# Thirty-two expert weights in 18 passes instead of 20: two passes of four experts, a pair at the end

## The reference, cut to what matters

```python
w_pair = g_w * jax.nn.softmax(top_v, axis=-1)        # two weights per token
e_id = g_sel[:, None] * EXPERTS_PER_GROUP + top_i    # two experts per token
# for each expert e and the rows xb of h that were sent to it:
hb = jax.nn.silu(xb @ w1[e]) * (xb @ w3[e])          # w1, w3: 1024 x 512
y  = (hb @ w2[e]) * w_b[:, None]                     # w2: 512 x 1024
# y of a token's two experts is added; then x + gate * rms_norm(sum)
```

## Time and profile before

| | us |
|---|---|
| median of 3 runs (lowest to highest) | 1152.71 (1152.04 to 1154.15) |
| the profiled execution | 1152.28 |
| its span | 1150.5 |
| first matmul of the expert stage, from the span's start | 610.71 |
| end of the last weight unit's matmuls | 1122.45 |
| PE busy in the span | 1041.2 (90%) |

### The profile page before, as it was taken

The page is one execution under the profiler, slowest core; times in us unless marked ns, Lnnn a source line. Parts: engine busy times, 40 slices in busy tenths (PEclk is TensorE's granted clock), DMA queues, the critical chain, the costliest instruction groups (busy, mean ns, idle before and its releaser), DMA issues. The chain is left out here.

```text
span 1150.5 us, 13873 instructions
## 1 busy us (share of the span) xinstructions
PE 1041.2 (90%) x5501; PEld 626.5 (54%) x5501; DVE 360.1 (31%) x646; ACT 285.0 (25%) x539; POOL 140.6 (12%) x221
## 2 busy tenths in 40 slices
PE   4999999999888898999968999997878979998896
PEld 2677778777766787878853333332323323333332
DVE  3553133112388885561582000100000000000006
ACT  4232213323377663122431010000000000100004
POOL 2122221000111301100221001000000000100000
PEclk9899999999989998999988999999999999999999
DMA  9634426544340213632578899999999999999954
GB/s 353 248 123 167 117 100 222 188 169 167 123 160 1 93 39 118 190 131 74 188 293 309 294 345 419 420 420 422 420 420 420 420 420 420 417 416 410 420 236 170
DMA packets 73845, 301.51 MB, mean 262 GB/s; under 512 B 8575, under 2 KB 14848, under 8 KB 48562
## 3 DMA queue, kind: packets, MB, share of 16 engines
q1 hardware_dynamic: 62064, 271.07, 60.6%
q0 software_dynamic: 11552, 29.46, 7.5%
q10 hardware_dynamic: 162, 0.05, 0.0%
HBM read 284.38 MB, written 26.38 MB: 270 GB/s over the span
## 5 line engine op out<-in xcount | busy, mean ns | idle before, releaser
L1367 PE MATMUL psum<-w_hi,act_hi 128*128 128x512 f32 (+1 forms) x480 | 188.6, 393 | 2.8 <-ACT rows L1156 1.4
L1369 PE MATMUL psum<-w_hi,act_lo 128*128 128x512 f32 (+1 forms) x480 | 183.9, 383 | 0.0
L1368 PE MATMUL psum<-w_lo,act_hi 128*128 128x512 f32 (+1 forms) x480 | 183.7, 383 | 0.0
L1769 PE MATMUL psum<-weights_ring,expert_x_columns 128*64 128x512 f32 x520 | 127.1, 613 | 11.1 <-DMA weights_ring<-in_w_e 8.7
L1302 ACT ACTIVATE expert_y<-psum 128x512 f32<-128x512 f32 x20 | 12.0, 598 | 460.9 <-PE psum L1780 460.9
L1769 PE MATMUL psum<-rows_ring,expert_x_columns 128*64 128x512 f32 x472 | 109.8, 603 | 7.3 <-DMA rows_ring<-in_w_e 7.3
L1367 PEld LDWEIGHTS psum<-w_hi,act_hi 128*128 128x128 f32 x480 | 90.9, 189 | 32.4 <-issue 14.2
L1369 PEld LDWEIGHTS psum<-w_hi,act_lo 128*128 128x128 f32 x480 | 90.8, 189 | 18.2
L1368 PEld LDWEIGHTS psum<-w_lo,act_hi 128*128 128x128 f32 x480 | 91.1, 190 | 16.3
L1894 DVE TENSOR_TENSOR w_lo<-raw_mix,w_hi 128x2048 fp32r<-128x2048 f32 (+1 forms) x24 | 52.9, 2202 | 148.4 <-ACT w_hi L1051 148.4
L1769 PEld LDWEIGHTS psum<-weights_ring,expert_x_columns 128*64 128x64 f32 x520 | 39.2, 140 | 79.1 <-issue 77.2
(11 more groups left out here) (352 smaller groups left out, 1303.2 us busy)
## 6 DMA issues: line engine op xcount, KB each, us to landing
weights_ring<-in_w_e SPq DMA_DIRECT2D x78, 1024.0 KB, 27.5
rows_ring<-in_w_e SPq DMA_DIRECT2D x75, 1024.0 KB, 27.6
raw_mix<-in_w_e SPq DMA_DIRECT2D x39, 1024.0 KB, 27.9
raw_mix<-in_w_in SPq DMA_DIRECT2D x16, 1024.0 KB, 5.8
raw_mix<-in_w_ada SPq DMA_DIRECT2D x16, 1024.0 KB, 7.0
ada_first<-in_w_ada SPq DMA_DIRECT2D x8, 1024.0 KB, 14.3
gates_scratch<-rows POOLq DMA_DIRECT2D x20, 256.0 KB, 3.3
y_scratch<-lam SPq DMA_DIRECT2D x1, 5120.0 KB, 16.8
```

The costliest lines, as they stand in the source:

```text
L1367: pe.matmul(out, a_hi(ka_), w_hi[:, kw, :], start=s, stop=False)
L1368: pe.matmul(out, a_hi(ka_), w_lo[:, kw, :], start=False, stop=False)
L1369: ins = pe.matmul(out, a_lo(ka_), w_hi[:, kw, :], start=False, stop=e)
L1769: ins = pe.matmul(out[x * w:(x + 1) * w, :], expert_xT[:, a:a + w], ring(slots[x % len(slots)])[:, kk * 512:(kk + 1) * 512], start=(k == 0 ...
```

## The change

The passes are 18. The first two take experts 0 and 1 by number. The other 30 go by rank: the 6 fullest alone, the next 16 in 8 pairs, the 8 emptiest in 2 passes of four experts (a quad), with 32 rows and 32 output columns for each. The quads are passes 3 and 13. The last three passes are pairs, the last one too. Its rows' weights are fetched: POOL writes the pair weights to memory and gathers those of the last pass by its index column. `loh` is made by DVE behind pass 1. The five reads of `y_d` stand in the list of loads, behind the last weights; the pair weights are stored interleaved.

```diff
-LEAD, ALONE, QUADS = 3, 4, 0
-PAIRS = (NE - LEAD - 1 - ALONE - 4 * QUADS) // 2
-RANKED = NE - LEAD - 1
-WIDTHS = [1, 1, 1, 2, 2, 1, 2, 2, 2, 2, 2, 1, 2, 2, 1, 2, 1, 2, 2, 1]
+LEAD, ALONE, QUADS = 2, 6, 2
+PAIRS = (NE - LEAD - ALONE - 4 * QUADS) // 2
+RANKED = NE - LEAD
+WIDTHS = [1, 1, 2, 4, 1, 2, 1, 2, 1, 2, 1, 2, 1, 4, 1, 2, 2, 2]
...
-    return units, loads
+    return units, loads + [(len(units), len(passes), 0, i, 0) for i in range(NT)]
...
-        PAIR_LOAD = len(moe_loads) - RING
+        PAIR_LOAD = load_no[NP, 0, 0, 0]
...
+            def load_pair(i):
+                sp.dma_start(raw_pair(i), y_d[2 * P * i:2 * P * (i + 1), :].rearrange("(p k) n -> p (k n)", k=2)).then_inc(x_in[i], 16)
+
             def ring_load(j):
                 _, p, m, u, x = moe_loads[j]
-                e = expert_number(*passes[p][x])
+                if p < NP:
+                    e = expert_number(*passes[p][x])
                 if j >= RING:
                     sp.wait_ge(moe_mm, moe_loads[j - RING][0] + 1)
+                if p == NP:
+                    if u == 0:
+                        sp.wait_ge(all_scattered, 1)
+                    load_pair(u)
+                    return
...
             all_experts()
-            sp.wait_ge(all_scattered, 1)
             pairs(0)
...
+            def last_slot_weights():
+
+                po.wait_ge(g2_in, 48)
+                po.sem_inc(row_dmas, 1)
+                po.indirect_dma_start(out=last_slot_w[:, :], out_offset=None, in_=wk_d,
+                                      in_offset=bass.IndirectOffsetOnAxis(pass_rows(tab_s, pass_s, NP - 1), 0),
+                                      bounds_check=last_pair, oob_is_err=False).then_inc(g2_in, 16)
...
+            po.wait_ge(last_weights, 2)
+            po.dma_start(wk_d.rearrange("(t p k) o -> p t (k o)", p=P, k=2), wk[:, :].rearrange("p (t k) -> p t k", k=2)).then_inc(g2_in, 16)
             for p in range(NP - 1):
                 if p + 2 < NP:
                     gather(p + 2)
+                if p == 0:
+                    last_slot_weights()
                 scatter(p)
...
-            pe.wait_ge(last_weights, 2)
-            parts = last_parts[:, :].rearrange("p (x n) -> p x n", n=3)
-            for x in range(2 * NT):
-                ins = pe.matmul(bank(7)[:, P:P + 3], roc[:, x * P:(x + 1) * P], parts[:, x, :], start=(x == 0), stop=(x == 2 * NT - 1))
-            ins.then_inc(last_weight_mm, 1)
...
-            link(ve.tensor_tensor(last_w[:, :], ohw[:, :].rearrange("p (x n) -> p x n", n=NE)[:, :, NE - 1], wk[:, :], ALU.mult))
-            link(ve.tensor_copy(parts[:, :, 0], last_w[:, :]))
-            link(ve.tensor_tensor(last_rest[:, :], last_w[:, :], parts[:, :, 0], ALU.subtract))
-            link(ve.tensor_copy(parts[:, :, 1], last_rest[:, :]))
-            link(ve.tensor_tensor(last_rest[:, :], last_rest[:, :], parts[:, :, 1], ALU.subtract))
-            ve.tensor_copy(parts[:, :, 2], last_rest[:, :]).then_inc(last_weights, 1)
...
             for p in range(NP):
                 gated_g(p)
                 g_columns(p)
                 y_half(p)
+                if p == 1:
+                    last_pass_onehot()
```

More of the change, by code:

```diff
@@ L87, in expert_passes @@
             passes.append([("number", p)])
-        elif p == len(WIDTHS) - 1:
-            passes.append([("number", NE - 1)])
         else:
@@ L256, in build @@
         wk = at("pair_weights", 2 * NT)
+        wk_v = wk[:, :].rearrange("p (t k) -> p t k", k=2)
         tab_s = at("scatter_rows", NE, U32)
@@ L358, in build @@
         y_d = nc.dram_tensor("y_scratch", (2 * TOK, D), F32).ap()
+        wk_d = nc.dram_tensor("pair_weights_scratch", (2 * TOK, 1), F32).ap()
         w_ada = t["w_ada"][0].rearrange("(k p) n -> p k n", p=P)
@@ L454, in build @@
         ol_done = sem("attention_lo_done")
-        b_tr = last_weight_mm = sem("modulation_transposed_or_last_weights_summed")
+        b_tr = sem("modulation_transposed")
         b_cp = sem("modulation_transposed_copied")
@@ L605, in build @@
         N_PAR = [sum(1 for p in range(NP) if p % 2 == x) for x in range(2)]
-        ring_loads = [sum(1 for j in range(len(moe_loads)) if j % RING == s) for s in range(RING)]
+        ring_loads = [sum(1 for j, x in enumerate(moe_loads) if j % RING == s and x[1] < NP) for s in range(RING)]
         def unit_end(p, m, u):
@@ L637, in h2_bank @@
             return 5 + j if i % 2 == 0 else j
-        PAIR_LOAD = len(moe_loads) - RING
+        PAIR_LOAD = load_no[NP, 0, 0, 0]
+        assert len(moe_loads) - PAIR_LOAD <= RING
         def raw_pair(i):
@@ L764, in pairs @@
                 for i in range(NT):
-                    if not again:
-                        sp.wait_ge(moe_mm, moe_loads[PAIR_LOAD + i][0] + 1)
-                    sp.dma_start(raw_pair(i), y_d[2 * P * i:2 * P * (i + 1), :].rearrange("(p k) n -> p (k n)", k=2)).then_inc(x_in[i], 16)
+                    if again:
+                        load_pair(i)
                 for i in range(NT):
@@ L958, in _ @@
             link(po.memset(xg[:, :], 0.0))
+            link(po.memset(last_slot_w[:, :], 0.0))
             last_row, last_pair = po.to_reg(TOK - 1), po.to_reg(2 * TOK - 1)
@@ L1302, in y_half, with first_part @@
                 ac.activation(ysb[:, par * D:par * D + 512], bank(5), ACT.Copy).then_inc(moe_ya, 1)
+            def first_part(i, again):
+                ac.wait_ge(x_in[i], 32 + 16 * again)
+                if not again and i == 0:
+                    ac.wait_ge(last_weights, 2)
+                y0 = raw_pair(i)[:, 0:D]
+                ac.activation(y0, y0, ACT.Copy, scale=wk[:, 2 * i:2 * i + 1]).then_inc(c_part, 1)
             x_columns_copied(0)
@@ L1321, in later_round @@
                     ac.activation(ysb[:, 0:512], bank(5), ACT.Copy).then_inc(moe_ya, 1)
[L1323 to L1326, removed]
             def pair_root(i, again):
@@ L1802, in transpose_x, with pair_rows @@
                 rows_transposed(p % 2).then_inc(moe_xt, 1)
+            def pair_rows(i):
+                pe.wait_ge(c_sum, i + 1)
+                for x in range(2):
+                    ins = pe.matmul(bank(SUM_BANK[i] + x), ident[:, :], raw_pair(i)[:, x * 512:x * 512 + 512], start=False, stop=True)
+                ins.then_inc(c_mm, 1)
             transpose_x(0)
@@ L1841, in _ @@
                     pe.matmul(bank(SUM_BANK[i] + x), loh[:, i * P:(i + 1) * P], ysb[:, LAST_PAR * D + x * 512:LAST_PAR * D + x * 512 + 512], start=True, stop=False)
[L1842 to L1845, removed]
+                pair_rows(i)
             def later_round(r):
@@ L2342, in _, with last_pass_onehot @@
             link(ve.tensor_tensor(later_pos[:, :], slot_pos[:, :], done_rows[:, :], ALU.subtract))
[L2344 to L2348, removed]
+            def last_pass_onehot():
+                ve.wait_ge(g2_in, 64)
+                link(ve.tensor_copy(last_tok[:, 0:1], pass_rows(tab_g, pass_g, NP - 1)))
                 link(ve.scalar_tensor_tensor(last_tok[:, 1:1 + NT], tokval[:, 2:2 + NT], -0.5, last_tok[:, 0:1].broadcast_to([P, NT]), ALU.mult, ALU.add))
@@ L2375, in _, with pair_sum @@
             ve.tensor_scalar(pass_g[:, :], pass_s[:, :], 1, None, ALU.logical_shift_right).then_inc(pass_done, 1)
+            ve.wait_ge(pass_done, 3)
+            def pair_sum(i, again):
+                ve.wait_ge(x_in[i], 32 + 16 * again)
+                ve.wait_ge(c_part, NT * again + i + 1)
+                y2 = raw_pair(i)
+                ve.scalar_tensor_tensor(y2[:, 0:D], y2[:, D:2 * D], wk[:, 2 * i + 1:2 * i + 2], y2[:, 0:D], ALU.mult, ALU.add).then_inc(c_sum, 1)
             for p in range(NP):
@@ L2395, in later_round @@
                     ve.tensor_copy(ysb[:, 512:D], bank(6)).then_inc(moe_yv, 1)
[L2397 to L2401, removed]
             def pair_gate(i, again):
```

13 lines of the change are left out of this document (3 added, 10 removed).

## The result

| | before | changed |
|---|---|---|
| median, us (lowest to highest) | 1153.43 (1152.04 to 1156.14), 4 runs | 1142.93 (1142.19 to 1144.40), 4 runs |
| ratio | | 0.9914, 95% interval 0.9900 to 0.9929 |
| profiled execution / its span | 1152.28 / 1150.5 | 1144.40 / 1142.7 |

What follows compares the result with a forecast made beforehand. PE bounds the front single passes and the end, the load stream (2.60 us per load) the stretch from 677-690 us. Terms -6.1 - 6.1 + 2.5 = -9.7 us give 1143.0 us, range 1139 to 1149 (own bounds 1139 to 1147).

Steps and rivals of the forecast that it cites:

- The stream fills earlier: Front passes: PE frees ring places sooner, so the weight stream is full from 654 instead of 677 us; -6.1 us.
- the upper bound: Largest gain allowed at the front: 677 to 690 us is filled too, 1.6 us more, 7.7 at most.
- 654 to 690 at about 420 GB/s: Profile sign at the front: transfers in this stretch run at full pace, else the gain from earlier filling fails.
- The last pass is a pair: End of stage: PE ends one unit behind the last load, 13.9 instead of 19.9 us after load 187; -6.1 us.
- The reads: Sums at the end: pieces of `y_d` follow the last load, piece 3 delays `pair_root(0)`; +2.5 us.
- Quads' matmuls: Passes of four experts: a unit takes 3.5 to 7 us, hidden under its loads' 10.4 us; 0 us.
- The clock did not reach the end: Rival: PE's lower clock after waits in quads holds on to the last unit and sums, 1159 us; 6%.
- The start of the stage: Before pass 2: later loads 10 to 12, later gather and the pair-weight write cost 0, at most +1 us.
- -5.2 and +5: Range's upper end: least gain from earlier filling with a loss at the end, put at 1146.7 us.
- PE's idle time in the stage: Profile sign in the expert stage: PE's idle time becomes twice as long, with waits between quad units.

Runs made afterwards that it cites:

- front as before: Changed kernel with the old order of widths at the front (three single passes first), still 18 passes and a pair last: 1148.83 us, ratio 0.9967.
- root earlier: Changed kernel with only ACT's order at the end altered, `pair_root(0)` behind `first_part(2)`: 1141.20 us, ratio 0.9906.
- reads last: Changed kernel with SP's reads of `y_d` also waiting for the end of the last down unit: 1151.31 us, ratio 0.9986.

## Why the prediction was right

The time and the mechanism were right, the time in part by luck: measured from G on, the front's gain was 1.8 us smaller than said, the last pass's 0.5 us smaller, and the reads cost 1.05 us less, which takes back nearly half of that.

- **The stream fills earlier: -6.1 said, -4.3 in the changed kernel's trace against that of before, -3.6 and -4.1 in the two pairs of experiments that differ in the front alone (G to L187).** The place and the cause were right: 5.6 us' worth of bytes are ahead at 88 us behind G. The sum behind it was right by two errors that cancel: the stream was full from some 667 on, not 654, so 654 to 677 gave (383 - 309) x 23 / 420 = 4.1 us, not 6.1, and 677 to 690, which stood in the upper bound alone, gave 1.8. The sign "654 to 690 at about 420 GB/s" was reached at 399 only. The step that failed is the silent one that the stream's lead there is still whole at the last loads. Against front as before, 1.96 of the 2.34 MB are left 486 us behind G (4.7 us), since SP's queue moved 158.77 MB in between against 159.15; why the full stream is 0.24% slower is open (158.89 MB, 0.16%, in root earlier and reads last). And load 187 lands 3.6 us earlier, not 4.7. The gap is there long before the end: load 100 lands 265.4 us behind G against 269.7, load 160 426.8 against 430.3. A reason that I only argue: bytes are a mean over 16 engines, and a load has landed when the slowest is through. The changed kernel's stretch from 1092 to 1104 shows them apart: a mean share of 0.49, while two loads still take 4.92 us (load 185, waited for until 1093.94, to load 187).

```profile
1092.00:1104.00 12.00, 8.67 (x40) 3.09 (x36) 1.38 (x2) 1.08 (x2) 0.99 (x1) 1.00 0.49 188
```

  By the medians the term is 5.9 and 5.6 us, each uncertain by some 2.4 us from the ratios' intervals. The medians alone would have confirmed the number; the traces from G on, which leave out the layer before it, do not.
- **The last pass is a pair: -6.1 said, -5.6 measured** (L187 to D, from 19.92 to 14.34; 14.18 to 14.35 in the seven kernels with a pair last). The four loads took 10.7 us (1098.86 to 1109.55), not 10.2.
- **The reads: +2.5 said, +1.5 measured** against before, and +2.0 to +2.3 against kernels with the same code and a single last pass. ACT waited for piece 3 as said, but the root came at D + 7.2, not D + 7.7: the pieces follow load 191 without a gap, as said, but 2.5 us apart, not 2.55, and D is 3.8 us behind its landing, not 3.7. The root is 2.0 us later than before, and this goes through to DVE's last instruction, which ends at D + 22.8 before and D + 24.7 now. The other 0.5 us lie behind it: 5.3 us to the end before, 4.8 now; why is open.
- **Quads' matmuls: 0, right.** A quad's unit (16 calls) takes 3.64 us in its record, as one of 64 columns does: four matmuls of 32 columns run side by side. (A unit of 64 columns is 8 calls; the 16 in the section on the kernel before is its number of records.) The unit behind a wait of 7.16 us starts with matmuls of 1.07 us instead of 0.59 (the lower of the two clock levels, 1.2 GHz) and is done 4.9 us after its start, at 706.0, as the clock rises within the unit; one behind a wait of 4.61 us takes 5.8. Both are hidden under the 10.4 us of the unit's loads. The Trainium skill, "TensorE: Matmul & The Clock Gate", Part 3, gives 2.38 times for three column tiles. Here four took the time of one matmul on all 128 columns (16 calls in 3.64 us, 0.86 us for one), and the measurement decides. The Trainium skill, same page, "HAM oscillation", agrees with the row of 701.07 in that the unit behind the wait starts at the lower clock. The clock did not reach the end: the granted clock is 1.00 from 1092 to the last matmul.
- **The start of the stage: 0 said, and "it cannot gain"; 0 measured.** Load 10 is issued 14.1 us later behind G than before and lands 16.3 us behind G, not 0.1. The cover held: load 23 lands 52.8 us behind G against 53.4, and PE waits for no weights before 701. The six DVE instructions and ten matmuls that go stood ahead of pass 0's transposes, which start 0.8 us earlier behind G, and I had counted them only for the expert numbers; but 0.1 us of it is left at pass 1. The write of the pair weights took POOL 0.91 us, with nobody waiting. The 0.7 us by which load 187 lands earlier with front and last pass put back (501.31 to 500.60) arise more than 88 us behind G, in the full stream, where I had put nothing; their cause is open.
- The sum from G is -4.32 - 5.58 + 1.45 = -8.45 us. The medians say -10.5, the ratio -9.9 (8.2 to 11.5 by its interval). So 1143.0 was met more closely by the median than by the terms. The profiled execution of the changed kernel is the slowest of its four runs, 1.5 us above their median, and that of before is 1.15 below its own: these 2.6 us are the scatter between executions, of which I have one trace each.

The upper end of my own range is off by a little: -5.2 and +5 give 1146.4, not 1146.7. One sign said beforehand was wrong: PE's idle time in the stage grew from 43.9 to 71.8 us (from 39.5 to 50.4 between 790 and 1092) and did not double. The stream's pace did not follow it, 419 GB/s before and 418 now.

## What to carry over

When a stream is the bound, ask two things of the work at its ends: where the consumer begins to free places faster than the stream needs them, and how much work stands behind the last load; both are settled by the order of the passes alone, and they add. The transfers that follow the stream belong into its list, behind the last load, and the queue of the engine that takes them up should put nothing that waits for the next piece ahead of what the next engine needs. And where executions differ ahead of the change, align the traces at the last instruction that it leaves alone before comparing them.

## What the runs showed that I had not expected

- Past G traces of the same passes repeat within some 0.5 us up to load 187, while G itself varies from 600.5 to 606.4: most of the scatter of the runs that I could see is made before the expert stage.
- Four 32-column matmuls side by side take what one on all 128 columns does: 16 in a unit whose record is 3.64 us.
- The kernels with two quads, the first as third or fourth pass, reach load 187 0.4 to 2.3 us later than those without (495.63 and 496.45 to 496.99 against 494.70 and 495.25), though no quad unit read here exceeds its loads' time. The number of passes and of single experts differs too, so that it is the quads is not shown. Some 0.3 us are PE's at pass 0, where 28 records of table matmuls take 1.19 us in all and 12 took 0.94; the rest was not found.
